# A table of slots in DRAM instead of index products, and an earlier branch of TensorE, in a diffusion step with routed experts

## The reference

```python
logits = t @ w_router                      # t: 640 x 1024, after the norm
top_v, top_i = top_k(logits, 2)
gates = one_hot(top_i) weighted by softmax(top_v)
y = sum over e of gates[:, e] * (silu(g_e) * u_e) @ w_down[e]     # g_e, u_e = split(t @ w_gu[e])
```

## Time and profile before

| what | us |
|---|---|
| median of three timed runs | 1994.7 |
| lowest and highest of them | 1992.4, 1995.81 |
| the profiled execution | 1990.26 |
| its span, first to last instruction | 1988.4 |
| TensorE busy in it | 1921.9 (97%) |
| VectorE busy in it | 1051.8 (53%) |
| ScalarE busy in it | 806.7 (41%) |
| layer 1: routing from norm 3's sums to the first index product | 1222 to 1252 |
| layer 1: from there to the first expert product | 1252 to 1271 |
| layer 1: the eight experts, with the turn of the last results | 1271 to 1963 |

### The profile page before, as it was taken

One profiled execution on the slowest core, in us unless ns is written; L12 is line 12 of the kernel. 1 busy time (PEld: TensorE's weight loads), 2 busy tenths in 40 slices (PEclk: granted clock), 3 DMA queues, 4 the chain that ended last, 5 costly groups with the idle time before them and its releaser, 6 DMA issues. The chain is left out here.

```text
span 1988.4 us, 30863 instructions
## 1 busy us (share of the span) xinstructions
PE 1921.9 (97%) x12773; PEld 1758.4 (88%) x12773; DVE 1051.8 (53%) x1637; ACT 806.7 (41%) x1295; POOL 108.2 (5%) x88
## 2 busy tenths in 40 slices
PE   7999989999999999999998899899999999999997
PEld 6999758999999999999996588799898988989885
DVE  2632675432232222346236754577676766768677
ACT  4321364432211222242213643555565655556564
POOL 2000000100000000110000001020000000002210
PEclk8999999999999999999998999999999999999999
DMA  8425101124231432305252010577776776768862
GB/s 345 181 79 212 54 1 68 60 96 169 87 117 43 182 115 75 117 22 191 72 206 52 1 39 32 164 221 225 235 244 213 220 226 215 231 214 262 295 198 64
DMA packets 91281, 290.46 MB, mean 146 GB/s; under 512 B 12820, under 2 KB 21396, under 8 KB 91136
## 3 DMA queue, kind: packets, MB, share of 16 engines
q1 hardware_dynamic: 84416, 270.15, 40.5%
q0 software_dynamic: 6720, 18.28, 2.8%
HBM read 281.97 MB, written 12.26 MB: 148 GB/s over the span
## 5 line engine op out<-in xcount | busy, mean ns | idle before, releaser
L1664 DVE TENSOR_TENSOR w_lo<-raw,w_hi 128x1024 fp32r<-128x1024 f32 x394 | 488.3, 1241 | 429.5 <-ACT w_hi L1200 418.4
L1200 ACT ACTIVATE w_hi<-raw 128x1024 fp32r<-128x1024 f32 x394 | 414.6, 1053 | 370.1 <-PE ps L679 179.3
L679 PE MATMUL ps<-a_hi,w_hi 128*128 128x320 f32 x1728 | 400.0, 313 | 9.1 <-DVE a_lo L1669 6.9
L679 PE MATMUL ps<-a_lo,w_hi 128*128 128x320 f32 x1728 | 394.2, 309 | 0.0
L679 PE MATMUL ps<-a_hi,w_lo 128*128 128x320 f32 x1728 | 394.0, 309 | 0.0
L1017 PE MATMUL ps<-hg,w_hi 128*128 128x416 f32 x1232 | 379.2, 365 | 0.8 <-DVE hg L2026 0.8
L1018 PE MATMUL ps<-hg,w_lo 128*128 128x208 f32 x1232 | 318.5, 259 | 0.0
L679 PEld LDWEIGHTS ps<-a_hi,w_hi 128*128 128x128 f32 x1728 | 287.2, 188 | 19.3 <-issue 14.7
L679 PEld LDWEIGHTS ps<-a_hi,w_lo 128*128 128x128 f32 x1728 | 289.5, 188 | 0.0
L679 PEld LDWEIGHTS ps<-a_lo,w_hi 128*128 128x128 f32 x1728 | 289.3, 188 | 0.0
L1018 PEld LDWEIGHTS ps<-hg,w_lo 128*128 128x128 f32 x1232 | 234.3, 190 | 0.5
(11 more groups left out here) (230 smaller groups left out, 2062.4 us busy)
## 6 DMA issues: line engine op xcount, KB each, us to landing
raw<-gu_w SPq DMA_DIRECT2D x220, 512.0 KB
raw<-moe_down_w SPq DMA_DIRECT2D x88, 512.0 KB
ada_raw<-ada_w SPq DMA_DIRECT2D x21, 2048.0 KB, 7.8
raw<-in_w SPq DMA_DIRECT2D x48, 512.0 KB
raw<-down_w SPq DMA_DIRECT2D x22, 512.0 KB
raw<-out_w SPq DMA_DIRECT2D x16, 512.0 KB
ada_pro<-ada_w SPq DMA_DIRECT2D x2, 2048.0 KB, 18.4
y_rows<-ey POOLq DMA_DIRECT2D x7, 512.0 KB, 3.7
```

What stands on the lines that cost most here:

```text
L679: ins = nc.tensor.matmul(out[:, hf, 0:HALF], w, o[:, hf * HALF:(hf + 1) * HALF], start=f, stop=e)
L1200: nc.scalar.activation(w_hi[:, s, :], raw[:, n % RAW, :], ACT.Copy).then_inc(hi_done, 1)
L1664: nc.vector.tensor_tensor(w_lo[:, s, :], raw[:, n % RAW, :], w_hi[:, s, :].bitcast(F32), ALU.subtract)\
```

## The change

The index products of experts 1 to 7 go, and with them their selections except expert 7's. In their place stands a table in DRAM, `slots_d`, of one number for each of the 8 x 208 slots. POOL zeroes it at the start of the kernel. After its branch it waits for the places, writes each token's number to its two slots (ten indirect transfers), and reads the table back as columns `slot_rows`, one per expert, in two strided transfers. From expert 1 on the fetches take their rows from there, and wait for the turn of the expert before. The condition rows of expert 7 are computed from the same table. The column sums of a norm are split: those of the seven added squares run ahead of the fills, which are five instead of nine, and those of the last square behind them. TensorE branches directly behind the index products; the turns of `x` and then those of the gathered rows stand behind the branch, without the four fills. `selection` reads the rank column in place, the rank's extra column is computed behind the first selection, and a clear moves ahead of the waits on token rows.

```diff
             out.append(("gu", e, c))
-            if e < LAST_E and c == 13:
-                out.append(("idx", e + 1, 0))
             if e == LAST_E and c in (5, 6):
                 out.append(("turn", e, c - 5))
...
+TURNED = {_e: _q + 1 for _kind, _e, _i, _q, _g, _c in MAIN if (_kind, _i) == ("tr", 1)}
...
-FILL = {"sums": 9, "spread": 5, "blocks": 13, "mask": 4, "ranks": 22, "gather": 4, "rows": 7}
+FILL = {"sums": 5, "spread": 5, "blocks": 13, "mask": 4, "ranks": 22, "rows": 7}
...
-            def sums_of(g, col, parts):
+            def sums_of(g, squares, first):
 
                 for t in range(TT):
-                    for squares in parts:
-                        ins = nc.tensor.matmul(ps[:, g % 4, 0, col + t:col + t + 1], squares[:, t * P:(t + 1) * P],
-                                               ones[:, 0:1], start=squares is parts[0], stop=squares is parts[-1])
-                ins.then_inc(mm_done, 1)
+                    ins = nc.tensor.matmul(ps[:, g % 4, 0, t:t + 1], squares[:, t * P:(t + 1) * P], ones[:, 0:1],
+                                           start=first and t == 0,
+                                           stop=not first and t == TT - 1)
+                return ins
...
             def norm_sums(i):
                 n0, q0, g0 = NORM_AT[i]
                 if i:
+                    open_block(g0)
+                pe.wait_ge(ss_add, KB * (i + 1) - 1)
+                sums_of(g0, ss[:], True)
+                if i:
                     fill(g0 + 1, FILL["sums"])
-                if i:
-                    open_block(g0)
                 pe.wait_ge(ss_add, KB * (i + 1))
-                sums_of(g0, 0, [ss[:], sq[:, (KB - 1) % 2, :]])
+                sums_of(g0, sq[:, (KB - 1) % 2, :], False).then_inc(mm_done, 1)
...
                             if kind == "idx":
-                                if e == 0:
-                                    fill(g0 + g + 1, FILL["ranks"])
-                                pe.wait_ge(sel_ready, e + 1)
-                                if e == 0:
-                                    pe.wait_ge(tok_ready, 1)
+                                fill(g0 + g + 1, FILL["ranks"])
+                                pe.wait_ge(sel_ready, 1)
+                                pe.wait_ge(tok_ready, 1)
                                 for st_ in range(ST):
                                     for t in range(TT):
...
                             elif kind == "tr":
                                 if i == 0:
-                                    if e == 0:
-                                        fill(g0 + g + 2, FILL["gather"])
                                     pe.wait_ge(gx_in, 16 * ST * (e + 1))
...
                             elif kind == "turn":
                                 pe.wait_ge(gates_ready, 1)
+                                pe.wait_ge(sel_ready, 2)
                                 ins = turn_slots(slot, i, e)
...
-                    main_expert(MAIN[:len(START)])
+                    main_expert(MAIN[:1])
                     pe.wait_ge(most_ready, 1)
                     with pe.If(pe.value_load(most_i[0:1, 0:1], min_val=0, max_val=T) > CAP):
+                        main_expert(MAIN[1:len(START)])
...
+            nc.gpsimd.memset(no_slot[:].bitcast(F32), 0.0).then_inc(ones_set, 1)
 
             def fetch_rows(e):
...
                     nc.gpsimd.indirect_dma_start(
-                        gx[0:ROWS[st_], st_, :], None, h_rows,
-                        bass.IndirectOffsetOnAxis(ap=slot_row[0:ROWS[st_], st_:st_ + 1], axis=0),
+                        gx[rows, st_, :], None, h_rows,
+                        bass.IndirectOffsetOnAxis(ap=slot_rows[rows, st_, e:e + 1] if e else slot_row[rows, st_:st_ + 1],
+                                                  axis=0),
                         bounds_check=T - 1, oob_is_err=False).then_inc(gx_in, 16)
+
+            def list_slots():
+
+                pool.wait_ge(places_ready, 1)
+                pool.wait_ge(slots_clear, 16)
+                for t in range(TT):
+                    for o in range(2):
+                        nc.gpsimd.indirect_dma_start(
+                            slots_d, bass.IndirectOffsetOnAxis(ap=early[:, o, t:t + 1], axis=0), tok_u[:, t:t + 1], None,
+                            bounds_check=EXPERTS * CAP - 1, oob_is_err=False).then_inc(slots_set, 16)
+                pool.wait_ge(slots_set, 16 * 2 * TT)
+                with nc.allow_non_contiguous_dma("one number per slot, once"):
+                    for st_ in range(ST):
+                        if st_:
+                            pool.wait_ge(slots_in, 16 * st_)
+                        nc.gpsimd.dma_start(slot_rows[0:ROWS[st_], st_, 1:EXPERTS],
+                                            slots_d.rearrange("(e c) o -> c (e o)", e=EXPERTS)
+                                            [st_ * P:st_ * P + ROWS[st_], 1:EXPERTS]).then_inc(slots_in, 16)
 
             def put_rows(e):
 
@@ -1603,6 +1634,7 @@
                             bounds_check=experts * CAP - 1, oob_is_err=False).then_inc(done, 16)
 
             def move_rows():
+                list_slots()
                 fetch_rows(1)
                 nc.gpsimd.memset(yab[:], 0.0).then_inc(zeroed, 1)
                 for e in range(LAST_E):
...
+            pool.wait_ge(ones_set, 4)
+            nc.gpsimd.dma_start(slots_d.rearrange("(p c) o -> p (c o)", p=P), no_slot[:]).then_inc(slots_clear, 16)
...
+                link(nc.vector.tensor_scalar(tokf[:], iot[:, 0:TT], float(P), pcol[:, 0:1], ALU.mult, ALU.add))
+                nc.vector.tensor_copy(tok_u[:], tokf[:]).then_inc(tok_set, 1)
...
                     dve.sem_inc(mask_ready, 1)
+                    link(nc.vector.memset(before[:, 0, :], 0.0))
                     for b in range(3, 2 + TT):
                         token_rows(b)
...
-                    link(nc.vector.memset(before[:, 0, :], 0.0))
...
-                    link(nc.vector.tensor_scalar(rank[:, :, EXPERTS:], rank[:, :, 0:1], float(CAP), None, ALU.subtract))
-
-                    def selection(e, count):
-
-                        nc.vector.tensor_copy(rcol[:], rank[:, :, e]).then_inc(rcol_set, 1)
-                        dve.wait_ge(rcol_set, count + 1)
+
+                    def selection(e, count=None):
+
+                        if count is not None:
+                            nc.vector.tensor_copy(rcol[:], rank[:, :, e]).then_inc(rcol_set, 1)
+                            dve.wait_ge(rcol_set, count)
                         for t in range(TT):
-                            ins = nc.vector.tensor_scalar(sel[:, t, :], iot[:], rcol[:, t:t + 1], None, ALU.is_equal)
+                            ins = nc.vector.tensor_scalar(sel[:, t, :], iot[:],
+                                                          rank[:, t, e:e + 1] if count is None else rcol[:, t:t + 1],
+                                                          None, ALU.is_equal)
                         ins.then_inc(sel_ready, 1)
...
-                                if f == 4 and e < LAST_E:
-
-                                    selection(e + 1, e + 1)
+                                if f == 4 and e == LAST_E - 1:
+
+                                    selection(LAST_E)
+                                    dve.wait_ge(slots_in, 16 * ST)
+                                    for st_ in range(ST):
+                                        rows = slice(0, ROWS[st_])
+                                        link(nc.vector.tensor_copy(cond_f[rows, st_:st_ + 1],
+                                                                   slot_rows[rows, st_, LAST_E:EXPERTS]))
+                                        link(nc.vector.tensor_scalar(cond_f[rows, st_:st_ + 1], cond_f[rows, st_:st_ + 1],
+                                                                     float(CTX), None, ALU.is_ge))
+                                        link(nc.vector.tensor_copy(cond_row[rows, st_:st_ + 1],
+                                                                   cond_f[rows, st_:st_ + 1]))
+                                    dve.sem_inc(cond_ready, 1)
...
-                    selection(0, 0)
+                    selection(0)
+                    link(nc.vector.tensor_scalar(rank[:, :, EXPERTS:], rank[:, :, 0:1], float(CAP), None, ALU.subtract))
                     link(nc.vector.tensor_reduce(most[:], before[:, TT, :], AX, ALU.max))
```

26 lines of the change are left out of this document (14 added, 12 removed).

## The result

In the runs that answer the prediction the changed kernel took 1981.29 us (median of eight, 1971.99 to 1987.32) and the kernel before 1991.78 (eight, 1987.87 to 1995.81) on the same chip: a ratio of 0.9939, 95% interval 0.9922 to 0.9955. It is faster, by 10.5 us where 11.6 were forecast, and the forecast of 1983.1 us is 1.8 us off. In a later set, with twelve runs of it and eighteen of before, the ratio was 0.9953 (0.9936 to 0.9969). The profiled execution took 1981.53 us (a span of 1979.7) against 1990.26 (1988.4).

A forecast was written before the change was run, and what follows sets the result against it. TensorE was taken to bound the kernel nearly everywhere. Index products 6.4, column sums 3.3 and branch 2.0, less 0.1 for a clear, made 11.6 us off the 1994.7 median: 1983.1 us, range 1977 to 1989.

The forecast's parts named there:

- What bounds the kernel: Nearly everywhere TensorE sets the time, busy 86.00 of 86.00 us in an expert stretch; three mid-kernel norms and expert-stage start differ.
- Index products, 6.4 us: Experts 1 to 7: seven groups at 0.92 us each leave TensorE's stream, 6.4 us less; lower bound 5.7.
- Condition rows: Expert 6, behind the remaining selection: VectorE's 26 us of slack per expert covers them; without cover about 1 us.
- Column sums, 3.3 us: Mid-kernel norms: five of ten sums run before the fills, reciprocal root's input 1.1 us earlier, 3 x 1.1; first norm 0.
- TensorE's branch, 2.0 us: Start of the expert stage: branch behind the index products, first product 2.8 us earlier, taken as 2.0 for the lower clock.
- a shorter branch away from busy DMA engines: Expert-stage start: TensorE's 3.85 us branch, moved where DMA engines idle, might shorten, making the sum 1.3 us larger; not counted.
- Slot table, 0: POOL, before expert 1: table written and read back, rows in 45 us after the places, cost 0; upper bound 1 us.
- some 10 us of cover: Expert 1's rows: in near 1309, wanted by TensorE at about 1321; past that cover each us is paid in full.
- Rival 3: Slot table late: strided reads hold expert 1's rows beyond 1321; with reads four times as long, about 2039 us; chance 0.05.
- Rank columns, 0: Chain to the first selection: two short VectorE steps and a clear leave it, but TensorE's 22 fills end last; worth 0.
- rival 1: Lower clock takes the expert-stage start's gain and catches norms 2 and 3; 1986.4 to 1988.6 us; chance 0.17.
- Rival 2: Experts don't give 6.4 us because weight splitting or DMA, hidden until now, paces; 1991 to 1994 us; chance 0.07.

The follow-up runs named there:

- 32 bytes on: Kernel before with 32 unused bytes per partition that move the large tiles 32 bytes; 1993.17 us, ratio 1.0025 to the kernel before.
- branch alone: Kernel before with only TensorE's branch moved behind the index products and the four fills behind it dropped; 1987.10 us, ratio 0.9999.
- table alone: Changed kernel, later tiles 512 bytes on, with the old column sums, nine fills and TensorE's branch at its old place; 1977.75 us, ratio 0.9952.
- sums alone: Kernel before with only the column sums split and five fills instead of nine; 1984.31 us, ratio 0.9983.
- all, 32 more: Changed kernel with 32 unused bytes behind its new tiles, so later tiles lie 192 bytes on; 1979.21 us, ratio 0.9956 to the kernel before.
- all, 512 bytes on: Changed kernel with a 352-byte pad behind its new tiles, so later tiles lie 512 bytes on; 1974.22 us, ratio 0.9932 to the kernel before.
- that, branch back: Changed kernel, tiles 512 bytes on, with TensorE's branch back behind the five turns of x, four fills still out; 1977.85 us, ratio 0.9933.
- that, places later: Changed kernel, tiles 512 bytes on, with VectorE's places moved behind the second split of the gathered rows; 1983.22 us, ratio 0.9978.
- that, 14 fills: Changed kernel, tiles 512 bytes on, with 14 instead of 22 fills ahead of expert 0's index products; 1974.15 us, ratio 0.9927.
- the three edits: Changed kernel with tiles 512 bytes on, expert 6's condition rows four chunks later and 14 fills for 22; 1974.14 us, ratio 0.9927 to the kernel before.

## Why the prediction was right, and where it wasn't

**What bounds the kernel**: right. TensorE is busy 86.00 of 86.00 us in the experts after, as before, and no wait on the splits grew, except in expert 6.

**Index products, 6.4 us**: the term is right to the hundredth (0.92 per period with the tiles in their old places). The step that failed is one that the working took for granted: that the products which stay keep their duration. Three small tiles declared ahead of the operands gave back 0.43 us per expert, some 3 us in all. Nothing in the trace of before shows it, but the diff shows that tiles are added.

**Condition rows**: "VectorE's 26 us of slack per expert covers that; without cover it would be about 1 us" was wrong by 0.4 us. The slack is an average; in one chunk of 2.4 us VectorE has the splitting of the weights, the products of the gate, the selection of 1.28 us and now six more steps. The cover has to be read from the chunk.

**Column sums, 3.3 us**: right by the runs (3.4, 0.6 to 6.2) and in the traces, 1.18 us in each of norms 2 and 3. Norm 1 gave 1.1 more in the profiled pair, because its spread ran at the full clock. The prediction named this as possible and took 0, and the kept traces lean the other way. A spread takes 1.34 us at full clock and 1.8 to 2.5 where it meets the lower level. How many of the spreads of norms 1, 2 and 3 were slow:

| column sums | traces | slow spreads of norm 1, 2, 3 |
|---|---|---|
| old: before, 32 bytes on, branch alone, table alone | 4 | 3, 2, 3 |
| split, five fills: all others | 10 | 2, 2, 0 |

With the sums split the lower level caught 4 spreads of 30 and not 8 of 12. Whether the order of the sums or the number of fills does it wasn't tested, nor whether the clock takes it back elsewhere.

**TensorE's branch, 2.0 us**: 1.7 in the profiled pair, but made up otherwise. The idle time was 2.79 us and not 3.9, since the branch starts while the index products still run. The turns of x then ran at a low clock, 7.37 us. Between the good case worked out, 16.1 us from the index products to the first product, which three versions show (15.8, 15.9 and 16.1), and the bad one, 20.2, lies the measured 17.2. Where it was 15.8 and 15.9, the fills ahead had run at the low clock instead (6.7 us). The places as next in line were right, and they do end last beside the landing of the rows. The wrong step is the credit: I gave the branch's new place all of what the four dropped fills brought. With the fills gone and the branch at its old place the ratio is the same, 0.9933 against 0.9932.

The prediction also weighed a shorter branch away from busy DMA engines. It misread the trace there: while the branch ran, the DMA share was 0.28 before (1260.60 to 1264.45) and 0.29 after (1249.40 to 1253.10), so that the two say nothing on this. The Trainium skill (Runtime: NRT & Kernel Launch, Instruction fetch mechanics) says that a taken branch out of the fetched pages has to wait for a DMA of its target; whether the DMA engines' load matters to it isn't shown. In other traces the branch took 3.35, 3.63 and 3.94 us at a share of 0.04 to 0.05, and 3.35, 3.61 and 5.27 (the kernel before, 32 bytes on) at 0.41, 0.32 and 0.50.

**Slot table, 0**: right in its sum, for a thinner reason. The rows of expert 1 were in some 49 us after the places, worked out 45; but the step "some 10 us of cover" became about 6, and the version with later places showed how fast it is used up: 4.87 us of waiting. The parts were off in both directions: two reads at 4 to 5 us each where I took 11.2, the landing of the writes 6.7 where I took 3 (the 5.5 to 11.2 us of the earlier trace rows are also of several kinds of transfer taken together), and a pause of 8 us that no row of before shows. The reading of the table was the wrong thing to fear; the writing of it is the long part. Rival 3 had a chance of 0.05, and with some 6 us of cover behind 49 of work it deserved more.

**Rank columns, 0**: right. The selection ended 2.4 us before the index products began, so the fills ended last. That was also the next thing to take, and taking it brought 1.5 us at the stage's start in a trace and nothing in the medians.

**Rivals**: rival 1, the clock, took part of the start's gain, behind the branch and ahead of the index products (1.6 us), but it didn't catch norms 2 and 3. It didn't decide, since norm 1, the attention of layer 1 and the last expert gained at least as much by the clock. Rival 2, the experts not giving their 6.4, came true in part (4.2, and 2.8 without the last expert's clock) but by a mechanism I hadn't listed: neither the splits nor the DMA engines, but the products themselves.

**Range**: its lower end doesn't follow from its terms. 1994.7 - 14.8 - 1.3 is 1978.6 and not 1977; the upper end, 1989, does follow from rival 1. The measured 1981.29 lies in both.

So the total agreed in part by luck: an unlisted loss of about 3.4 us (tiles, condition rows) stood against gains that weren't counted, from the four fills and from the clock in norm 1 and in the last expert. In the version with the tiles 512 bytes on the ratio is 0.9932, 13.5 us.

## What to carry to other kernels

Where TensorE is the bound, an instruction taken out of its stream is worth its duration in the chain; but look also at what the change moves in memory: compare the duration of products that it doesn't touch, and declare new small tiles behind the large operands or pad them to where those lay. Read cover from the one chunk in which the new work stands, not from an engine's average, and for a chain that moves through DMA writes, reads and fetches, take each hop from a row and try what a few us of delay do. When several edits meet in one stretch, ask which of them frees it once the others are in: here the dropped fills rather than the moved branch, as far as the traces tell. A total that comes out as forecast doesn't show that its terms do: compare the stages one by one, and look in several traces before a difference in the clock is put down to the change.

## What the hardware showed that I had not expected

The speed of the expert products depends on where their operands lie: down products 30.46 us per 132 at 0, 192 and 512 bytes on, 30.66 and 30.71 at 32 and 160; gate and up stages 52.79 at 0 and 512 and 52.95 to 53.10 at 32, 160 and 192, with all else the same.

Four of the eight runs of the changed kernel lie more than 0.3% from their median, so the 0.3% said at the outset is too narrow here. The scatter goes mostly with the granted clock. The changed kernel's fastest run, 1971.99 us, had a mean clock of 0.993 and its slowest, 1987.32, one of 0.986. Over 169 runs of all versions, each taken from its version's mean, a line through time against clock falls by 1.28 us per 0.001 of clock, and about it runs scatter by 1.8 us, not 3.4. On that line, at a clock of 0.989:

| version | us at 0.989, mean | standard error |
|---|---|---|
| before (74 runs) | 1987.6 | 0.2 |
| sums alone | 1983.7 | 0.5 |
| branch alone | 1986.7 | 0.6 |
| table alone | 1978.9 | 0.3 |
| before, 32 bytes on | 1991.9 | 0.6 |
| the changed kernel, first eight runs | 1980.7 | 0.9 |
| the changed kernel, the twelve later | 1979.3 | 0.5 |
| all, 32 more | 1979.2 | 0.5 |
| all, 512 bytes on | 1975.8 | 0.7 |
| that, branch back | 1976.4 | 0.4 |
| that, places later | 1981.5 | 1.0 |
| that, 14 fills | 1975.5 | 0.9 |
| the three edits | 1975.4 | 0.5 |

This is worked out after the fact, and it hides what an edit does to the clock itself. It agrees with the ratios: 3.9 for the sums, 8.7 for the table, 0.9 for the branch, 0.6 for its place once the fills are gone, 3.5 for the places of the tiles. The first three add up to 13.5 where the version with 512 bytes has 11.8: a surplus of 1.7, about what the four fills brought, which are in two of them.

On POOL, small indirect writes go out every 1.29 us, but the eighth stands behind a pause of 7.5 to 11.1 us, in each of the ten traces with the table. What it waits for isn't shown by a releaser and wasn't tried.
